# First feed-forward's down projection by seven block products of even and odd row tiles, with GpSimd splitting the weights

## The reference

```python
v = rmsnorm(h, norm_ffn_w[l])
gate = causal_depthwise_conv(v @ w_gate[l], conv_w[l], conv_b[l])      # D_FF = 2816
h = h + (jax.nn.silu(gate) * (v @ w_up[l])) @ w_down[l]                # the down projection
return rmsnorm(h, final_norm_w)                                        # then: second block
...
h = rms_norm(x, mix_pre_g[l])          # second block begins
z = h @ w_in[l]
```

## Time and profile before

| | before |
|---|---|
| median of 3 runs | 2699.9 us (2699.8 to 2702.14) |
| the profiled execution | 2701.41 us, span 2699.7 us |
| PE busy | 98% of the span |
| POOL busy | 54% |
| DVE busy | 54% |
| ACT busy | 33% |

### The profile page before, as it was taken

One profiled execution on the slowest core, in us unless ns is written; L12 is line 12 of the kernel. 1 busy time (PEld: TensorE's weight loads), 2 busy tenths in 40 slices (PEclk: granted clock), 3 DMA queues, 4 the chain that ended last, 5 costly groups with the idle time before them and its releaser, 6 DMA issues.

```text
span 2699.7 us, 33443 instructions
## 1 busy us (share of the span) xinstructions
PE 2643.5 (98%) x12923; PEld 2155.2 (80%) x12923; DVE 1445.9 (54%) x1977; ACT 891.1 (33%) x1417; POOL 1462.6 (54%) x1440
## 2 busy tenths in 40 slices
PE   8999999999999999999999999999999999999998
PEld 6989866888888888888787777878667888887887
DVE  4587874665545423635414434448578766663132
ACT  4354463332112211222113334334464322222032
POOL 4741403768777687855331121355225877875873
PEclk9999999999999999999999999999999999999999
DMA  6432333312222263445635332533021222236442
GB/s 237 156 133 86 118 109 117 133 47 94 94 83 87 97 242 141 164 67 133 176 98 123 98 129 80 204 109 110 32 78 54 103 78 79 79 106 223 148 155 96
DMA packets 185972, 316.69 MB, mean 117 GB/s; under 512 B 7396, under 2 KB 116303, under 8 KB 185815
## 3 DMA queue, kind: packets, MB, share of 16 engines
q1 hardware_dynamic: 137728, 214.45, 25.5%
q10 hardware_dynamic: 48087, 100.11, 10.4%
HBM read 235.85 MB, written 78.68 MB: 117 GB/s over the span
## 4 chain that ended last, share of the span: by engine, by line
PE 84%; DVE 9%; ACT 2%; issue 2%; POOL 2%; DMA 1%; ACTq 0%; DVEq 0%; SPq 0%; POOLq 0%
PE PS L1033 26%; PE PS L292 22%; PE PS L1047 16%; PE PS L1761 5%; PE PS L2964 3%; PE PS L1767 2%; PE PS L2561 2%; PE PS L2639 1%; PE PS L2627 1%; PE PS L2611 1%; PE PS L1816 1%; DVE SC L651 1%; POOL WL L3683 1%; DVE SC L2365 1%; PE PS L581 0%
## 5 line engine op out<-in xcount | busy, mean ns | idle before, releaser
L3679 POOL CAST WH<-raw 128x512 fp32r<-128x512 f32 (+1 forms) x240 | 183.6, 779 | 862.5 <-issue 640.5
L292 PE MATMUL PS<-UH,WH 128*128 128x512 f32 x1040 | 426.9, 411 | 9.9 <-DVE UL L732 3.6
L292 PE MATMUL PS<-UH,WL 128*128 128x512 f32 x1040 | 407.3, 392 | 0.0
L292 PE MATMUL PS<-UL,WH 128*128 128x512 f32 x1040 | 407.1, 391 | 0.0
L3683 POOL TENSOR_TENSOR WL<-raw,WH 128x512 fp32r<-128x512 f32 (+1 forms) x240 | 336.6, 1413 | 0.0
L1585 POOL TENSOR_TENSOR WL<-raw,WH 128x512 fp32r<-128x512 f32 x176 | 256.5, 1468 | 0.0
L292 PEld LDWEIGHTS PS<-UH,WH 128*128 128x128 f32 x1040 | 196.2, 189 | 69.1 <-issue 15.4
L1033 PE MATMUL PS<-UL,WH 128*128 128x512 f32 x640 | 249.2, 389 | 1.9 <-ACT SC L1142 1.0
L1033 PE MATMUL PS<-UH,WH 128*128 128x512 f32 x640 | 249.1, 389 | 1.1 <-DVE SC L1298 0.9
L1033 PE MATMUL PS<-UH,WL 128*128 128x512 f32 x640 | 249.0, 389 | 0.0
L292 PEld LDWEIGHTS PS<-UL,WH 128*128 128x128 f32 x1040 | 196.5, 189 | 42.3 <-issue 4.8
(11 more groups left out here) (422 smaller groups left out, 5763.0 us busy)
## 6 DMA issues: line engine op xcount, KB each, us to landing
raw<-in_w_down SPq DMA_DIRECT2D x44, 1024.0 KB, 6.2
raw<-in_w_up SPq DMA_DIRECT2D x33, 1024.0 KB, 5.2
raw<-in_w_in SPq DMA_DIRECT2D x27, 1024.0 KB, 9.0
act_rows<-SC SPq DMA_DIRECT2D x22, 1024.0 KB, 4.0
ULf<-act_rows SPq DMA_DIRECT2D x28, 512.0 KB, 4.1
raw<-in_w_gate SPq DMA_DIRECT2D x11, 1024.0 KB, 5.4
raw<-in_w_out SPq DMA_DIRECT2D x8, 1024.0 KB, 5.1
xres<-XTf ACTq DMA_DIRECT2D x16, 512.0 KB, 2.8
```

The source lines that it names most:

```text
L292: mm = pe.matmul(PS[:, banks[f], :], w[:, k, f * P:(f + 1) * P], u[:, k, half(h)], start=(k == 0 and j == 0), stop=(k == n_k - 1 and j == 2))
L3679: pool.tensor_copy(wh[slot][:, cols], raw[slot % 2][:, cols]).then_inc(hi_done[slot], 1)
```

## The change

The down projection becomes seven block products instead of eight. The 2816 rows are divided into even and odd row tiles (11 of each), the 1024 output columns into two halves, the tokens into two halves. Each of the seven products has 11 steps (`STEPS` = 77); a step is one row tile (or a sum or difference of two) for 4 output tiles and 512 tokens: 4 x 3 = 12 matmuls (`step`). Their weight operands are halves of rows of `w_down` or sums and differences of two halves, made on DVE in `raw` (`step_sum`, products 0, 2, 3, 4 and 6). Their activation operands are rows, differences (`step_difference`, product 1), or one of four sums, which DVE makes for each group in the up phase (`act_sums_of`, four instructions) and SP stores to the new DRAM tensor `act_sums`. Each product's four banks are added to one or two of the four quarters of `XT` (`step_add`). `raw` is now used as four places of 1024 columns, and POOL casts and subtracts 512 columns for each step. The norm of half 0 moves to the last products and its `split` behind the last `step_low`; both `renew` and both `keep` stand at the end.

```diff
@@ FFN
+            STEPS = 7 * FG
+            F1, F2 = 1, 0
+            ADDS = (((F2, 0, 1), (F2, 1, -1)), ((F1, 0, 1), (F2, 0, 1)), ((F1, 0, 1), (F2, 1, 1)), ((F1, 0, 1),),
+                    ((F1, 0, -1), (F1, 1, 1)), ((F1, 1, 1), (F2, 1, 1)), ((F2, 1, 1),))
...
+            def step_done(self, n):
+                i, j = n // FG, n % FG
+                return self.y_full(4 * i + 4) if j == FG - 1 or n >= self.STEPS - 3 else self.d_full(10 * i + j + 1)
...
+            def step(self, pe, n, ms=range(4)):
...
+                if ms[0] == 0:
+                    pe.wait_ge(*self.rows_ready(n + 1))
+                    pe.wait_ge(*self.a_low(n + 1))
+                for m in ms:
+                    bank = self.BANK[4 * (i % 2) + m]
...
+                    for q, (w, u) in enumerate(((H, uh), (H, ul), (L, uh))):
+                        mm = pe.matmul(PS[:, bank, :], w[:, m * P:(m + 1) * P], u, start=(j == 0 and q == 0), stop=(j == FG - 1 and q == 2))
...
             def down_first(self, pe):
...
+                for n in range(self.STEPS - 3):
+                    self.step(pe, n)
+                    if n == 6 * FG + 3:
+                        pe.wait_ge(*self.y_free(22))
+                        self.then.add_up_both(pe, 0)
+                last = range(self.STEPS - 3, self.STEPS)
+                for m in range(4):
+                    for n in last:
+                        self.step(pe, n, (m,))
+                pe.wait_ge(*self.y_free(28))
@@ scalar, behind the ring
-                act.wait_ge(*then.joined_weights(1))
-                for m in range(KT):
-                    act.wait_ge(*self.y_free(m + 1))
-                    then.square_both(act, 0, m)
-                ring_high(FG + 5)
-                then.rstd_both(act, 0)
-                then.high(act, 0, range(KT))
+                for n in range(2, self.STEPS):
+                    step_high(n)
...
+                    if 72 <= n < 76:
+                        act.wait_ge(*self.y_free(20 + n - 72 + 1))
+                        then.square_both(act, 1, n - 72, n - 68)
                 then.rstd_both(act, 0)
                 then.high(act, 0, range(KT))
...
+                then.keep(act, 0)
                 then.keep(act, 1)
@@ vector
+                for n in range(2, self.STEPS):
+                    if n == 4:
+                        act_sums_of(FG - 1)
+                    if n + 2 < self.STEPS:
+                        step_sum(n + 2)
+                    if n + 1 == FG:
+                        step_difference(FG)
+                    if FG <= n + 1 < 2 * FG and n + 1 > FG:
+                        step_difference(n + 1)
+                    step_low(n)
...
+                    i, m = divmod(n - 13, FG)
+                    if n >= 13 and m < 4:
+                        step_add(i, m)
...
+                then.accumulate_both(dve, 1, 3)
+                then.split(dve, 0, range(KT))
+                for m in range(4):
+                    step_add(6, m)
                     if m >= 1:
+                        then.accumulate_both(dve, 1, 3 + m)
...
+                for h in range(2):
+                    dve.wait_ge(*then.lo[h](KT))
+                    then.renew(dve, h, range(KT), sums=False)
@@ sync
+                    if not self.second:
+                        sp.wait_ge(*self.act_sum(4 * g + 4))
+                        sp.dma_start(sums[:, :, g, :], sc(0, 2 * T).rearrange("p (a t) -> p a t", a=4)).then_inc(self.act_stored.sem, 16)
...
+                    for n in range(6):
+                        step_acts(n)
+                    for n in range(4, self.STEPS + 2):
+                        if n < self.STEPS:
+                            step_rows(n)
+                        if n == 6:
+                            store_acts(FG - 1)
+                        if n >= 8:
+                            step_acts(n - 2)
+                        if 8 <= n < 12:
+                            residual(n % 2, n // 2 - 4)
@@ gpsimd
+                    step_high(0)
+                    for n in range(1, self.STEPS):
+                        step_high(n)
+                        step_low(n - 1)
+                    step_low(self.STEPS - 1)
```

272 lines of the change are left out of this document (214 added, 58 removed).

## The result

The changed kernel takes **2715.95 us** (median of 3 runs, 2715.83 to 2720.21), against 2699.9 before: 1.0061 times as long, with a 95% interval of 1.0046 to 1.0075. In a second series, beside 15 runs of the kernel before, it took 2718.03 us (5 runs), 1.0066 [1.0052, 1.0080]. The forecast was 2699, about the time before, with 2683 to 2720 as its range: the time lies in the range, but 17 us above the forecast, and the kernel became slower by more than the interval leaves open. The profiled execution took 2720.21 us, 4.3 more than the median.

The account below looks back on a forecast made before the run. PE's own work was taken to bound the kernel, POOL next. From the profiled 2701.41 us, -29.9 - 4.7 + 7 + 11 + 14 + 1 + 0.5 gave 2700.3, or 2699 against the median; range 2683 to 2720.

Parts of the forecast that it names:

- Matmuls and the old waits, -29.9 and -4.7: Down projection: 132 fewer matmuls at 0.2267 us save 29.9 us; waits of chunks that no longer exist save 4.7.
- The first group and the up phase, +0.5: Up phase: activation sums lie hidden in DVE's gaps, except at the first group, where gaps are shorter: 0.5 us.
- The start, +11: First steps of the down projection: PE waits for loads queued behind the `act_sums` store; 11 us, bounds 6 and 15.
- The steady pace, +7: Down projection steps: DVE and POOL share SBUF time; additions 1.1 us in four products, accumulations 2.8; together 7 us.
- The common time of 206 us: Down projection: 73 POOL pairs and 162 DVE instructions share 206 us of SBUF time, as long as PE's 202.7.
- DVE's queue sets the pace: Rival, products 1 to 4 and 6: each DVE instruction waits for one of POOL's; steady 24, 2716 us; chance 0.29.
- The end, +14: Before the second block's first matmul: PE waits for half 0's `split`, additions and accumulations; 14 us, bounds 9 and 19.
- E - 7.5: Forecast start of half 0's `split`: 7.5 us before E, the end of the down projection stage.
- If `split` starts early enough, the last wait is short: Sign of being wrong: half 0's `split` starts early enough for the wait before the second block to be short.
- Behind it, +1: Second block: half 0's `renew` ahead of half 1's delays ACT emptying PSUM; PE waits 1 us, range 0 to 3.

Follow-up runs that it names:

- e6: Kernel before, with only the up phase's four activation sums a group and their stores added, down projection left as it was: 2702.04 us, 1.0004.
- f4: Changed kernel with residual loads ahead of the activations of steps 4 and 5, and the last `act_sums` store three steps later: 2708.72 us in the profiled execution.
- f2: Changed kernel with f4's edits, and ScalarE instead of GpSimd rounding the weights, behind the same step's high part: 2689.33 us.
- e9: Changed kernel with two tiles of half 0's `split` ahead of product 6's additions, six tiles and the accumulations behind; PE's last wait 13.3 us, median not stated.
- e3: Changed kernel with half 0's reciprocal root behind step 73, `split` two tiles a step from step 74, PE waiting for three of four additions: 2714.68 us.
- ctl_changed: The changed kernel itself, unedited, run again in a second series beside the kernel before: 2718.03 us, 1.0066.

## Why the prediction was wrong, step by step

It foresaw no change that could be told from none, and 16 us were lost. It had the three places and the engines right, and each place cost more than its term; only for the pace was the way in which the loss is made wrong.

- **Matmuls and the old waits, -29.9 and -4.7: right.** 924 matmuls at 0.2267.
- **The first group and the up phase, +0.5: right.** The stage begins 0.3 us later, and e6 is 1.0004 of before.
- **The start, +11: measured 17.2, above the upper bound of 15.** The mechanism was right: waits ahead of steps 4 to 11 (forecast from step 5), released by DVE's low parts, SP's stand behind `act_sums`, then the lump of loads; f4 and f2 bear it out. Its size failed. Step 10 was to be ready at 984.5 and began at 990.03. Of these 5.5 us, 1.5 are SP's stand (959.0 for 957.5) and 2.3 the rate, taken from single slices as 425 GB/s where the trace holds about 388; some 1.7 stay open. Behind that start another 1.7 us go to matmuls at the 1.2 GHz level.
- **The steady pace, +7: measured 10.4 in steps 12 to 73 without the ones, and 5.0 in steps 74 to 76.** This is the largest miss, and the step that failed in its mechanism. The common time of 206 us, "as long as PE's, with nothing over", is not contradicted, since most steps run at 2.72 us. What failed is the way from that mean to a loss. The additions were put at 1.1 us a product; in steps 12 to 41 all losses together were 2.9. The accumulations were put at 0.465 each, 2.8 in all; 12.5 us are lost from step 42 on, where they stand. There GpSimd is not in alternation with DVE, as the earlier trace rows had it, but stands still for 5.22 us, and squares and accumulations hold up a high part. By its size this is near the rival *DVE's queue sets the pace*, decided at 2.96 us a step: the mean over steps 12 to 76 is 2.72 + 15.4 / 65 = 2.96. Its mechanism, each DVE instruction waiting for one of POOL's, is not what happened: the losses come in bursts, and in them POOL waits for DVE.
- **The end, +14: measured 17.7, within 9 to 19.** Order and releaser were as forecast. `split` began at E - 4.8 rather than E - 7.5, since ScalarE's last high parts stood behind squares, and took 14.4 rather than 16.5 us; the additions with the accumulations between them took 7.9 rather than 5, beside GpSimd's split. What the step did not see is the second chain, GpSimd's for the next weights, which makes 13.3 us in e9. "If `split` starts early enough, the last wait is short" was therefore right only in part: e3, with `split` begun earlier, still waits 7.8.
- **Behind it, +1: measured 2.9** (0.7 in ctl_changed). The term was for ScalarE emptying PSUM later, behind both `renew`; no wait of PE for it shows in the new profile between 1208.5 and 1400 us, so the mechanism was wrong. What does show is the clock: the second block's first matmuls start 0.43 us apart, the 1.2 GHz level, up to 1212.01, which makes 2 us that stood in no term.
- The differences are 6.2 + 8.4 + 3.7 + 1.9 - 0.2 = 20.0, and 2700.3 + 20.0 = 2720.3, where the profiled execution took 2720.2. This must come out, since the account divides the whole of that execution; it shows that nothing was left out, and not that each cause is right.

## What to carry to other kernels

When a change leaves two engines with as much common work as the bound engine has time, a sum of means says "nothing over". Look for the few steps where a third task joins them, because there the loss is made and nothing gives it back. Move work to an engine with time over, but put it behind, not ahead of, the instruction that the others wait for: against ctl_changed the same rounding made the kernel 28 us slower ahead of it and 17 faster behind. A wait in the profile names only its last releaser: before its chain is shortened, work out when the next one ends.
